# Two residual joints of a two-block network: the first token block's product issued before the second block is turned

## The reference

```
h = h + gate * y                                  # residual
u = rms_norm(h, g) * (1 + scale) + shift          # per token, then per column
p = u @ w_in                                      # dense product, 1024 deep
```

## Time and profile before

| | us |
|---|---|
| median of three executions | 1146.14 |
| lowest, highest | 1143.59, 1146.99 |
| the profiled execution, own time | 1148.44 |
| its span, first to last instruction | 1146.6 |

### The profile page before, as it was taken

How to read it: one execution, slowest core, us unless ns; L and a number is a source line. 1 busy time by engine, 2 the same in 40 slices (tenths; PEclk the granted TensorE clock), 3 DMA queues, 4 the chain that set the end, 5 groups by cost and what they waited for, 6 DMA issues and landing times.

```text
span 1146.6 us, 11092 instructions
## 1 busy us (share of the span) xinstructions
PE 925.8 (81%) x4392; PEld 481.4 (42%) x4392; DVE 297.5 (26%) x536; ACT 212.3 (19%) x451; POOL 46.3 (4%) x98
## 2 busy tenths in 40 slices
PE   4999989999798989666665665656668899998997
PEld 2666454754544555121111221112213584643673
DVE  2299233591351352000000000000002114421022
ACT  2223221221363222000000000000002214401021
POOL 0200000000200100000000000000000000000000
PEclk9999989999999989888888889797898999998999
DMA  9954542692787449999999999999999106413200
GB/s 351 344 199 147 184 147 74 233 354 74 281 299 293 174 172 402 430 428 429 429 427 428 429 429 428 428 429 428 428 429 401 48 1 220 147 44 122 73 1 37
DMA packets 65336, 310.20 MB, mean 271 GB/s; under 512 B 2722, under 2 KB 4949, under 8 KB 52885
## 3 DMA queue, kind: packets, MB, share of 16 engines
q1 hardware_dynamic: 62836, 301.04, 65.8%
q0 software_dynamic: 2464, 8.68, 2.2%
HBM read 308.66 MB, written 1.05 MB: 270 GB/s over the span
## 4 chain that ended last, share of the span: by engine, by line
PE 60%; DMA 29%; DVE 5%; ACT 2%; issue 2%; SPq 1%; POOL 1%; POOLq 0%; DVEq 0%; ACTq 0%
PE bank L817 36%; DMA ring<-w_up_dram 27%; PE bank L1179 9%; PE bank L836 3%; PE bank L1429 2%; DMA ring<-w_in_dram 2%; PE bank L1342 1%; PE bank L964 1%; PE bank L847 1%; PE bank L1197 1%; PE bank L1348 1%; PE bank L1210 1%; PE bank L1364 1%; PE bank L826 1%; PE bank L1016 1%
## 5 line engine op out<-in xcount | busy, mean ns | idle before, releaser
L1179 PE MATMUL bank<-ring,ilat 128*32 128x512 f32 x960 | 146.1, 764 | 107.3 <-DMA ring<-w_up_dram 107.3
L1179 PEld LDWEIGHTS bank<-ring,ilat 128*32 128x32 f32 x960 | 39.7, 135 | 211.2 <-issue 211.2
L817 PE MATMUL bank<-ring,kT 128*128 128x512 f32 (+1 forms) x224 | 101.2, 614 | 5.8 <-ACT kT L1459 2.2
L817 PE MATMUL bank<-ring,hT 128*128 128x512 f32 x224 | 97.2, 593 | 0.0
L2249 DVE TENSOR_TENSOR state<-state,bank 64x512 f32<-64x512 f32 x16 | 11.0, 690 | 323.9 <-ACT state L1682 323.9
L817 PE MATMUL bank<-hT,ring 128*128 128x256 f32 (+1 forms) x320 | 88.0, 436 | 4.0 <-DVE hT L1875 2.0
L1197 PE MATMUL bank<-ring,ilat 128*32 128x512 f32 x512 | 67.5, 674 | 11.4 <-ACT ilat L1686 11.4
L817 PEld LDWEIGHTS bank<-hT,ring 128*128 128x128 f32 x320 | 62.5, 197 | 28.7 <-issue 21.5
L1682 ACT ACTIVATE state<-bank 64x512 f32<-64x512 f32 x16 | 9.5, 592 | 329.0 <-PE bank L1179 329.0
L817 PEld LDWEIGHTS bank<-ring,kT 128*128 128x128 f32 x224 | 44.6, 201 | 60.5 <-issue 60.5
L1210 PE MATMUL bank<-state,ilat 128*128 128x512 f32 x120 | 55.5, 605 | 12.3 <-DVE state L2253 12.3
(11 more groups left out here) (341 smaller groups left out, 982.5 us busy)
## 6 DMA issues: line engine op xcount, KB each, us to landing
ring<-w_up_dram SPq DMA_DIRECT2D x32, 2048.0 KB, 23.2
ring<-w_gate_dram SPq DMA_DIRECT2D x32, 2048.0 KB, 18.7
ring<-w_down_dram SPq DMA_DIRECT2D x32, 2048.0 KB, 23.8
ring<-w_ada_dram SPq DMA_DIRECT2D x24, 2048.0 KB, 11.2
ring<-w_in_dram SPq DMA_DIRECT2D x8, 2048.0 KB, 13.4
ring<-fno_w_in_dram SPq DMA_DIRECT2D x4, 2048.0 KB, 19.2
ring<-w_out_dram SPq DMA_DIRECT2D x2, 2048.0 KB, 8.5
ring<-mla_w_in_dram SPq DMA_DIRECT2D x2, 2048.0 KB, 18.0
```

The lines of the kernel that those rows point to most:

```text
L817: ins = pe.matmul(o, l, r, start=start and i == 0, stop=stop and i == len(terms) - 1)
L1179: ins = pe.matmul(bank[0][32 * t:32 * t + 32, :], x[:, j, :], w[2 * half + t // 2][:, j % JH, n0:n0 + TN], start=j == 0, stop=j == J - 1)
```

## The change

On PE, a helper `turn_block(tag, b, normed)` waits for one normalised block and issues its transposes; `block_turned(tag, b)` waits until that block's two banks are written to `u2T`.

Second residual: after block 0 is turned, the first four chunks of `("pa", 0)` are summed, then block 1's transposes are issued, then the last four chunks; `("pa", 1)` follows. DVE and ACT keep their order there.

Third residual: block 0's transposes are issued ahead of the last `y2` product. Then come `("fz", 0, 0)`, block 1's transposes, `("fz", 0, 1)`, `("fz", 1, 0)` and `("fz", 1, 1)`. ACT and DVE write the turned chunks of a block straight after that block's squares or normalisation, so those of block 0 stand ahead of the residual work of block 1.

```diff
-            for b in range(TB):
-                pe.wait_ge(sem("x2_normed"), b + 1)
+            def turn_block(tag, b, normed):
+                pe.wait_ge(sem(normed), b + 1)
                 for g in range(2):
-                    turn_chunks(("x2T", b, g), xn[:, b, :], g)
+                    turn_chunks((tag, b, g), xn[:, b, :], g)
+
+            def block_turned(tag, b):
+                for g in range(2):
+                    wait_copied(pe, (tag, b, g))
+
+            turn_block("x2T", 0, "x2_normed")
             w = wait_tile(pe, ("min", 0), J, 448)
-            for b in range(TB):
-                for g in range(2):
-                    wait_copied(pe, ("x2T", b, g))
-            for b in range(TB):
-                tokens_out(("pa", b), w, u2T, b, 448)
+            block_turned("x2T", 0)
+            o = pe_take(pe, ("pa", 0))
+            sum_of(o[:, 0:448], [(u2T[:, j, 0:P], w[:, j, :]) for j in range(4)], stop=False)
+            turn_block("x2T", 1, "x2_normed")
+            fills(sum_of(o[:, 0:448], [(u2T[:, j, 0:P], w[:, j, :]) for j in range(4, J)], start=False), ("pa", 0))
+            block_turned("x2T", 1)
+            tokens_out(("pa", 1), w, u2T, 1, 448)
...
                 for n in range(2):
+                    if (b, n) == (1, 1):
+                        turn_block("x3T", 0, "x3_normed")
                     tokens_out(("y2", b, n), wait_tile(pe, ("mout", n)), oT, b)
...
-            for b in range(TB):
-                pe.wait_ge(sem("x3_normed"), b + 1)
-                for g in range(2):
-                    turn_chunks(("x3T", b, g), xn[:, b, :], g)
-            for b in range(TB):
-                for g in range(2):
-                    wait_copied(pe, ("x3T", b, g))
+            block_turned("x3T", 0)
+            wf = [wait_tile(pe, ("fin", n)) for n in range(2)]
+            tokens_out(("fz", 0, 0), wf[0], u2T, 0)
+            turn_block("x3T", 1, "x3_normed")
+            tokens_out(("fz", 0, 1), wf[1], u2T, 0)
+            block_turned("x3T", 1)
             for n in range(2):
-                w = wait_tile(pe, ("fin", n))
-                for b in range(TB):
-                    tokens_out(("fz", b, n), w, u2T, b)
+                tokens_out(("fz", 1, n), wf[n], u2T, 1)
...
             for b in range(TB):                                   # ScalarE
                 residual_norm(2, b)
-            turned_modulated(("x3T",), u2T, FNO)
+                turned_modulated(("x3T",), u2T, FNO, bs=[b])
...
             for b in range(TB):                                   # VectorE
                 add_branch("y2", 2, b, 0)
                 normalise(2, b, "x3_normed")
-            turned_modulated(("x3T",), u2T, FNO)
+                turned_modulated(("x3T",), u2T, FNO, bs=[b])
```

More of the change, by code:

```diff
@@ L1828, in input_norm, with turned_modulated @@
                                            ALU.mult), "normed")
-            def turned_modulated(tag, dst, s, t0=0):
-                for b in range(TB):
+            def turned_modulated(tag, dst, s, t0=0, bs=range(TB)):
+                for b in bs:
                     name = tag + (b, 1)
```

## The result

Four executions of the changed kernel took 1134.94 to 1138.33 us, median 1137.57, beside a median of 1145.61 for the kernel before on the same chip. The ratio is 0.9923, with a 95% interval of 0.9900 to 0.9946: 8.0 us faster (6.2 to 11.5). The forecast was 1136.6, range 1133.0 to 1141.0.

What follows compares the result with a forecast made beforehand. The prediction took PE, busy for 81% of the span, as the bound. Gains of 9.0 us at the third residual and 0.5 at the second, 9.5 together, from the median 1146.14 gave 1136.6 us, range 1133.0 to 1141.0.

Steps and rivals of the forecast that it cites:

- Third residual, 9.0 us from 38.24 - 29.2: Third residual: block 0's first transposes to first gate record shrink from 38.24 to 29.2 us, gaining 9.0 us.
- nothing shows that the joints differ between executions: Both joints: the gain from the profiled execution, 1148.44 us, was taken unchanged from the median, 1146.14 us.
- cover: Third residual: DVE's 2.5 us delay hides under 5 us; the first `fz` product covers block 1's chain with 2.5 us slack.
- Transposes between products, 0.88 us: Both joints: a block's eight transposes standing right behind products hold PE's stream for 0.88 us.
- The rival by which they would: Three new places: transposes between products drop the clock, costing 11.1 us against 9.5 gained; 1147.7 us, chance 0.02.
- Second residual, start 1.40 us sooner: Second residual: the product begins at 893.06, 1.40 us earlier, since it waits only for block 0's turned chunks.
- Second residual, the same dip as before (3.4 us at half rate): Second residual: low clock again lasts 3.4 us, losing 1.7 us, so the joint gains 0.5 us net; chance 0.56.
- the bounds given, 2.2 and -0.6: Second residual: gain of 2.2 us if the clock doesn't fall, -0.6 us if low clock also lies under the transposes.
- Sum: Both joints: 9.0 us at the third residual plus 0.5 us at the second make 9.5 us.

Runs made afterwards that it cites:

- third-only kernel: The change with PE's order at the second residual as before; 1136.77 against 1145.19 us for the kernel before, ratio 0.9918.
- two partial kernels: The change with ACT and DVE at the third residual as before, ratio 1.0013; the change with only block 0's transposes early on PE there, 1.0012.
- variant with both turns in the pause: The change with block 1's transposes straight behind block 0's in the second residual's pause; run twice, 1134.33 us (ratio 0.9898) and 1133.72 us (0.9899).
- second alone: The change with PE, ACT and DVE at the third residual as in the kernel before; ratio 0.9997 to the kernel before.
- the one with fillers: The change plus five matmuls of constants behind block 0's transposes in the second residual's pause; 1134.87 us, ratio 0.9899 to the kernel before.

## Why the forecast held, point by point

- *Third residual, 9.0 us from 38.24 - 29.2.* Right: 9.03, and 9.03 again in the third-only kernel, both against the same profile of before; its parts were 5.13 us of idle time (5.10 forecast) and 3.90 of busy time, nearly all low clock (3.7). That it came out to 0.03 us is luck: the profile of before had 10.2 us of low clock at this joint, and beside the second profile of the same order, with 6.8, the gain is 8.03. The forecast left that out ("nothing shows that the joints differ between executions"). No cover was used up. Block 0's transposes followed the third `y2` product without a wait; its chunks on DVE put block 1's first half 2.2 us back (2.5 forecast), hidden; block 1's normalisation ended 4.13 us behind the last `y2` (4.15), with 2.5 us of slack (2.5).
- *What makes the gain there.* The forecast put it down to PE's gaps and the clock. The two partial kernels show which edits it needs together: a product of block 0 ahead of block 1's transposes, and ACT and DVE serving block 0 before block 1. Without the queues the joint is 65.31, without the new order of products 65.65, with both 56.76; the order of before takes 64.79 or 65.79. What block 0's transposes would cost behind the last `y2` product instead of ahead of it wasn't run.
- *Transposes between products, 0.88 us.* Right, 0.87 at all three places. They didn't drop the clock: 1.00 over 1001 to 1060, and behind those of the second residual 1.00 up to 957 in all five profiles of this order. The rival by which they would is refuted here.
- *Second residual, start 1.40 us sooner.* It was 1.67: 3.68 us behind the first transpose instead of 5.35. The chunks of block 0 ended as forecast; the issue behind them took 0.09 us in the chain of the change and 0.35 in that of before.
- *Second residual, the same dip as before (3.4 us at half rate).* This term was mis-sized. In the change's order the low clock cost 3.05 us (profile of the change), 1.4 twice and nothing twice, where before it cost 1.7. The net of the joint was thus between 2.5 us gained and 0.6 lost, with 0.5 forecast; the bounds given, 2.2 and -0.6, were about right, and the low one came true because the clock fell before the product began and stayed low for 6.8 us, not because the transposes ran slowly (1.07 us). The mean of the five joints is 17.85, a gain of 1.3 us, but five profiles are few.
- *The clock behind one and the same pause.* In five profiles of one order it cost 0, 1.4 and 3.05 us. The Trainium skill, "TensorE: Matmul & The Clock Gate", part 1, says that the schedule on which the chip judges TensorE's activity isn't aligned with the kernel, so that the number of slow matmuls of one kernel varies from run to run; the five profiles agree. Part 4 of the same page of the Trainium skill says that transposes don't count as activity as products do. The variant with both turns in the pause is no support for that, nor against it: eight more transposes there, and no low clock in two profiles. In the kernel before and the third-only kernel the same transposes stood in the pause, and the clock fell, but there the product came 1.7 us later. The variant has both a shorter idle stretch and more work; which of them keeps the clock, or whether it was chance, isn't separated.
- *Sum.* 9.5 forecast, 8.0 timed (6.2 to 11.5). The two joints of the profiles give 9.03 - 0.57 = 8.46. The second edit can't be seen in the time: third alone 8.4 us faster, whole change 8.0 and 7.6, second alone no difference (interval 1.3 us slower to 1.9 faster).
- *MLA between the joints* took 97.3 us in three profiles (the change, third alone, first run of both turned in the pause) and 99.0 in the other seven; the change and the variant are in both groups. The difference of 1.65 us isn't the change's. It is the clock at one place: in the seven long ones it stood at 1.2 GHz for 3.4 us somewhere between 962 and 970, under a group of attention scores (L1342 in the kernel before, 3.19 us instead of 1.72) and its neighbours, and in the three short ones it stayed at 2.4 GHz there.

## What to carry to other kernels

At a joint of two blocks, look for a product that needs only the first block and is longer than the chain that finishes the second (6.9 us against 4.1 here), and then change every queue that serves it: PE's new order without the helpers' was worth nothing. Transposes that are ready during a pause belong into the pause, not between the halves of the next product; that variant had the second joint at 15.8 us against 16.7 to 19.7 and, with 1133.7 and 1134.3 us, was the fastest kernel, beside the one with fillers (1134.9), which can't be told from it. Of that advantage 0.88 us are shown to come from the place of the transposes; the rest is the clock, which may have been chance. Where a pause of PE ends in products, price the clock as a range, not as the one stretch that a single profile shows; that holds for the profile before the change as well.

## What the runs showed of the hardware

One instruction order left three different clocks behind the same pause of 2.6 us: full clock, 1.2 GHz for about 3.4 us, and 1.2 GHz for 6.8 us. In the longest case the clock fell 0.7 us ahead of the product (891.3) and came back after 6.2 us of unbroken matmuls (898.1). The same pause filled so that PE stood for 0.43 us ahead of the product left none, in one profile. In the third-only kernel the clock fell 1.4 us into the product. At the third residual the order of before had 10.2 us of low clock in one profile and 6.8 in another. The time up to the first transpose of the second residual, where no kernel differs from another, varied from 887.4 to 890.7 us between profiles, which is more than the second edit could ever be worth.
